# Gate products and squares of a chunked scan on GpSimd in place of VectorE, and five weight splits at other steps of the attention beside it

## What is computed

```python
proj = rms_norm(x, norm_w) @ w_in
z, xbc, dt, q, k, v, g = split(proj)
y = ssd_chunked_scan(xs, dt, A, bm, cm) + d_skip * xs     # 256 x 1024
y = y * silu(z)                                           # gate product
y = rms_norm(y.reshape(256, 4, 256), ssd_norm_w)          # squares, sums, root
o = dilated_attention(q, k, v) * silu(g)                  # 8 heads, 3 dilations
x = x + concat([y, o]) @ w_out                            # 1536 x 1024
```

## Time and profile before

| what | before |
|---|---|
| median of 3 runs | 1747.39 us |
| lowest, highest run | 1747.34, 1750.71 us |
| the profiled execution, its own time | 1747.27 us |
| its span in the trace | 1745.2 us |
| TensorE busy | 1704.9 us, 98% of the span |
| VectorE busy | 1254.9 us, 72% |
| ScalarE busy | 961.1 us, 55% |
| GpSimd busy | 22.7 us, 1% |

### The profile page before, as it was taken

The page is one execution under the profiler, slowest core; times in us unless marked ns, Lnnn a source line. Parts: engine busy times, 40 slices in busy tenths (PEclk is TensorE's granted clock), DMA queues, the critical chain, the costliest instruction groups (busy, mean ns, idle before and its releaser), DMA issues. The chain is left out here.

```text
span 1745.2 us, 28417 instructions
## 1 busy us (share of the span) xinstructions
PE 1704.9 (98%) x10546; PEld 1487.7 (85%) x10546; DVE 1254.9 (72%) x2290; ACT 961.1 (55%) x1622; POOL 22.7 (1%) x21
## 2 busy tenths in 40 slices
PE   7999999999999999999999999999999999989998
PEld 6888899998888888888899988888888987878887
DVE  6666777567876667666776667866677799696775
ACT  5444555666555446444655665555556555574474
POOL 1000000000000000000000000000000000000000
PEclk9999999999999999999999999999999999999999
DMA  7545555634545554455555544455544444203531
GB/s 315 188 180 191 203 196 181 234 141 182 183 184 201 192 205 169 181 186 201 192 191 221 190 145 182 181 183 194 200 182 181 181 162 164 109 38 145 211 115 61
DMA packets 29904, 311.59 MB, mean 179 GB/s; under 512 B 3312, under 2 KB 3696, under 8 KB 4848
## 3 DMA queue, kind: packets, MB, share of 16 engines
q1 hardware_dynamic: 28944, 307.13, 47.5%
q0 software_dynamic: 864, 3.15, 0.5%
HBM read 309.21 MB, written 1.05 MB: 178 GB/s over the span
## 5 line engine op out<-in xcount | busy, mean ns | idle before, releaser
L505 ACT ACTIVATE region_r<-ring 128x1024 fp32r<-128x1024 f32 x505 | 525.1, 1054 | 360.1 <-PE psum L923 335.5
L511 DVE TENSOR_TENSOR ring_r<-ring,region_r 128x1024 fp32r<-128x1024 f32 x496 | 592.4, 1221 | 128.6 <-ACT region_r L505 123.6
L923 PE MATMUL psum<-xs_r,region_r 128*128 128x256 f32 (+2 forms) x3160 | 580.0, 331 | 3.2 <-ACT region_r L505 1.4
L923 PEld LDWEIGHTS psum<-xs_r,region_r 128*128 128x128 f32 (+1 forms) x3160 | 466.4, 188 | 65.8 <-issue 7.7
L923 PE MATMUL psum<-region_r 128*128 128x512 f32 (+3 forms) x1056 | 330.7, 381 | 0.0
L923 PE MATMUL psum<-xs_r,ring_r 128*128 128x256 f32 x2344 | 317.6, 278 | 0.0
L923 PEld LDWEIGHTS psum<-xs_r,ring_r 128*128 128x128 f32 x2344 | 303.9, 188 | 15.8
L923 PE MATMUL psum<-region_r,xs_r 128*128 128x512 f32 (+2 forms) x1056 | 272.8, 351 | 6.0 <-DVE region L2771 3.0
L923 PEld LDWEIGHTS psum<-region_r 128*128 128x128 f32 (+2 forms) x1056 | 193.1, 185 | 36.4 <-DVE region_r L2441 0.6
L923 PEld LDWEIGHTS psum<-region_r,xs_r 128*128 128x128 f32 x1056 | 185.6, 191 | 34.5 <-DVE region L2771 4.3
L923 PE MATMUL psum<-ring_r,region_r 128*128 128x512 f32 (+1 forms) x472 | 169.5, 376 | 0.0
(11 more groups left out here) (253 smaller groups left out, 1538.2 us busy)
## 6 DMA issues: line engine op xcount, KB each, us to landing
ring<-in_weights SPq DMA_DIRECT2D x192, 1536.0 KB, 6.3
gpost<-in_posts POOLq DMA_DIRECT2D x6, 512.0 KB, 4.5
cst<-in_const SPq DMA_DIRECT2D x1, 1165.0 KB, 22.7
PTs<-in_mem SPq DMA_DIRECT2D x1, 1024.0 KB, 5.6
x<-in_x SPq DMA_DIRECT2D x1, 1024.0 KB, 8.1
out<-x SPq DMA_DIRECT2D x2, 512.0 KB, 2.6
pars<-in_par SPq DMA_DIRECT2D x1, 368.0 KB, 6.1
p<-in_par SPq DMA_DIRECT2D x1, 206.0 KB, 22.7
```

The source lines that it names most:

```text
L505: eng.activation(unit.high, unit.like_high(unit.raw), ACT.Copy).then_inc(h_ready, 1)
L511: eng.tensor_tensor(unit.like_high(unit.low), unit.like_high(unit.raw), unit.high.bitcast(F32), ALU.subtract)\
L923: ins = pe.matmul(bank, lhsT, rhs, start=start, stop=stop)
```

## The change

The two gate products and the two squares leave VectorE's steps 1 to 4 and become four instructions of GpSimd, behind its last low part. GpSimd waits for all four banks of the scan to be emptied and for `z_ready`; a square waits for its product by the new semaphore `y_gated`, and VectorE's sum of squares at step 5 waits for the new `y_squared` in place of its own. The low parts of units 2 to 6, made at steps 6 to 10 before, are made at steps 3, 4, 6, 7 and 8.

```diff
@@ GpSimd, behind its last low part
             lows([U_EVEN + AHEAD_N - 1])
+
+            all_emptied(pool, [("scan", j) for j in range(4)])
+            pool.wait_ge(z_ready, 1)
+            for i in range(NT):
+                pool.tensor_tensor(ysb[:, i], ysb[:, i], Z[:, i, :], ALU.mult).then_inc(y_gated, 1)
+            for i in range(NT):
+                pool.wait_ge(y_gated, i + 1)
+                pool.tensor_tensor(yt[:, i], ysb[:, i], ysb[:, i], ALU.mult).then_inc(y_squared, 1)
@@ VectorE, y_steps
                 if s == 0:
                     scanned(1)
-                elif s in (1, 2):
-                    if s == 1:
-                        all_emptied(dve, [("scan", j) for j in range(4)])
-                    dve.wait_ge(z_ready, 1)
-                    own(dve.tensor_tensor(ysb[:, s - 1], ysb[:, s - 1], Z[:, s - 1, :], ALU.mult))
-                elif s in (3, 4):
-                    own.settle()
-                    own(dve.tensor_tensor(yt[:, s - 3], ysb[:, s - 3], ysb[:, s - 3], ALU.mult))
                 elif s == 5:
-                    own.settle()
+                    dve.wait_ge(y_squared, NT)
                     dve.tensor_reduce(stat[:, 0, 0:8], yt.rearrange("p i (g d) -> p (i g) d", g=4), AX.X, ALU.add)\
                         .then_inc(y_sq, 1)
...
-                if 6 <= s <= 9:
-                    low_part(dve, U_EO + s - 4)
+                if s in (3, 4, 6, 7, 8):
+                    low_part(dve, U_EO + (3, 4, 6, 7, 8).index(s) + 2)
                 elif s == 10:
                     mixed_low(8)
-                    low_part(dve, U_EO + 6)
```

More of the change, by code:

```diff
@@ L756, in build @@
         y_sq, y_std, y_ready = sem("y_sq"), sem("y_std"), sem("y_ready")
+        y_gated, y_squared = sem("y_gated"), sem("y_squared")
         trig_in, trig_done = sem("trig_in"), sem("trig_done")
```

## The result

The changed kernel takes 1750.43 us (median of 9 runs, 1750.15 to 1754.97) against 1747.77 for the kernel before in the same comparison (9 runs, 1747.18 to 1750.71): a ratio of 1.0022, 95% interval 1.0014 to 1.0030, or +2.7 us. Its profiled execution took 1753.06 us, with a span of 1751.1; it is already 2.34 us late where the dilated attention begins, which is the difference of two executions and not the change's. So the lengths of one piece are compared from here on: from the start of TensorE's scores of head 0 to its first transposes of the scan output. It contains all that the change touches but the low part of step 10, which stood right behind it; behind it both traces have 179.9 us to their end. In the kernel before it runs from 1525.55 to 1565.34, 39.79 us; after, from 1527.89 to 1571.20, 43.31: **+3.52 us**.

A forecast was written before the change was run, and what follows sets the result against it. TensorE, busy 98% of the span, was taken as the bound, with 4.4 us idle to win. Turns made head 1's transposes 4.06 us late; partial recovery left +2.6 on 1747.39, so 1750.0 us, range 1745.2 to 1751.7.

The forecast's parts named there:

- step 4: Dilated attention: VectorE's scalings and GpSimd's four instructions wait for each other's whole instructions; TensorE ends +2.6 us late.
- rival A: GpSimd also blocks the 128x2 scaling L2547 between front and pair: +3.2 to +3.7 us, about 1751.0; chance 0.23.
- step 3: GpSimd's four added instructions, 2.35 us each, 9.4 in all, start 0.08 us after the last scan bank is emptied.
- The first pair: Head 0's two L2568 scalings wait for GpSimd's first and second products, ending at 1535.09 us instead of 1532.48.
- The second pair: Head 1's two L2568 scalings wait for both GpSimd squares, ending at 1540.23 us; TensorE's transposes come 4.06 us late.
- VectorE's lateness in the middle: VectorE 3.43 us late from head 4's front on; TensorE's idle 0.79 us at head 7's scores shrinks to 0.16.
- The end: TensorE's idle 0.83 us before the stretch's end disappears, as VectorE's last scaling ends at 1567.57 and TensorE's outputs at 1567.94.
- Rival B: Scalings take no turn with GpSimd, or the pair keeps the path: faster within 0.2%, 1745.1 to 1746.1 us; chance 0.20.
- C: Nearly all 4.4 us of TensorE's idle time in the dilated attention goes: 1743.0 to 1743.8 us; chance 0.04.
- D: VectorE's late steps fall into TensorE's pace, so the time does not change, +-0.5 us; chance 0.05.

The follow-up runs named there:

- run with uncut products: Fitted run with GpSimd's two gate products as whole 128x1024 tiles behind the last scan bank, VectorE squaring: 1750.03 us, ratio 1.0013.
- the fitted one: The change with gate products on GpSimd cut into four halves placed early, squares back on VectorE, low parts at steps 6 to 8 and the end: 1746.23 us.
- relief alone: The change with the gate products and squares left out altogether, made by no engine: 1747.14 us, ratio 0.9994.
- clock kept up: The change plus 18 identity transposes on TensorE while it waits ahead of head 0's transposes: 1751.78 us, ratio 1.0027.
- the run with one column: The change with the 128x2 scaling of the maxima written as two of 128x1 in the dilated attention: 1752.48 us, ratio 1.0019.
- the one with the low parts back: The change with VectorE's low parts of output weights back at steps 6 to 10: 1753.51 us, ratio 1.0040.
- the one with less work on VectorE: Fitted run with ScalarE squaring and summing tile 1 of the scan output, VectorE's low parts up to two steps sooner: 1744.91 us, ratio 0.9986.
- VectorE late alone: Fitted run plus two overwritten reductions on VectorE ahead of head 0's pair of scalings: 1749.04 us, ratio 1.0009.
- the transposes put in: 18 identity transposes in TensorE's wait, added to the change (1751.78 us), to uncut products (1749.48) and to VectorE late alone (1747.03).

## Why the prediction was right, and where not

The number was right: 1750.0 forecast, 1750.43 measured, +2.6 against +2.7 (interval +2.4 to +5.2). The ratio, 1.0022, lies just over the 0.2% that the prediction took as its bound, so on the side to which it gave 0.27 and not 0.68, with the interval over both. The mechanism of step 4 holds: whole instructions of GpSimd and VectorE take turns, scalings too. The run with uncut products against the fitted one shows it with the amount held the same. But the sum came out by errors that cancel, which is luck: the course was the first half of rival A, whose own sign (L2547 of head 1 at about 1 us) came true with 1.08, and the piece's +3.52 lies in A's +3.2 to +3.7, though by the half clock that A did not have.

| the piece from head 0's scores, us | length | against before |
|---|---|---|
| before | 39.79 | |
| relief alone | 38.09 | -1.70 |
| GpSimd's turns added, clock kept up | 42.45 | +2.66 |
| the change | 43.31 | +3.52 |

- **The start (step 3).** GpSimd takes up the signal of the last emptied bank 0.26 us after it (1532.10 to 1532.36), not 0.08. Products take 2.36, as taken from the earlier trace rows; the squares, which read one tensor twice, 2.07 and not 2.35. So the second square ends at 1541.11 - 2.34 = 1538.77 in the time of the trace of before, where the forecast had 1539.89.
- **The first pair (step 4).** It should have waited for the rest of the first product and, between its two scalings, for the second. The 128x2 scaling before it was held, which is the first half of rival A; that cost 0.91 us and let the second product ahead of the pair. Idle 4.49 us, not 2.5. The prediction's reason against A, that two columns hardly need a second path, is what failed: two do, one doesn't (0.21 us in the run with one column).
- **The second pair.** Forecast: held by both squares, transposes of head 1 4.06 us late. Shown: free, since the squares had ended 0.12 us before it. The whole loss sits at head 0; the transposes of head 1 are 4.46 late (15.14 against 10.68 us from the scores of head 0), 3.62 in the run with the clock kept up.
- **VectorE's lateness in the middle.** Forecast 3.43, with the idle 0.79 shrinking to 0.16. Shown: as late as TensorE, 4.4 us (the sum of squares at 1554.23, less 2.34, against 1547.47), and 0.75 left. The step set VectorE's front of head 4 at the very end of its scores; it starts 0.58 us behind them (scores to 1547.10, front at 1547.68), and 0.58 in the relief alone too (1541.95, 1542.53). In the trace of before 0.63 lay between (1540.29, 1540.92), but there VectorE's own square filled it. With 0.58 put in, VectorE is as late as TensorE and the idle 0.79 cannot shrink. What the 0.58 us are was not tried.
- **The end.** The idle 0.83 us disappears, as forecast, in every run but the one with the low parts back, where it stays.
- **The half clock** stood nowhere in the prediction: 0.86 us of the 3.52.

Without it the piece has grown by 2.66 us, the forecast's 2.6: TensorE is 3.62 us late at head 1's transposes and not 4.06, and makes up 0.96 of it and not 1.46.

Of the signs that the prediction named, these came: the pair of head 0 far over 0.48 us a scaling, the gap at the end gone, no wait for the squares. These did not: the later instructions of GpSimd at 2.5 us or more (2.36 and 2.07), the pair of head 1 held, the idle time of 2.5 us twice (4.49 once, and nothing at head 1).

**Rival B**'s walk of the relief alone gave -2.3 where -1.70 was measured: head 3's scores come 0.74 us sooner and not 0.9, and the idle 0.79 keeps 0.74. **C** fell with it: with four instructions off VectorE and nothing on GpSimd's side, 2.5 us of idle time remain (0.76, 0.74, 1.04). **D** is excluded by the interval.

What stays open: the medians scatter about the difference of the pieces by up to 2.1 us (most in the run with the low parts back, whose interval of +4.5 to +9.4 leaves its piece's +4.08 just out; the other nine hold theirs). Other parts of the program vary from one execution to the next, also by the clock (below).

## What to carry to other kernels

Before work goes to GpSimd beside VectorE, list which of VectorE's instructions would share a path with it and on which of them another engine waits; then cut and place GpSimd's instructions between those: here the same two products cost 4.8 us (2.3 of them half clock) or nothing. A blocked instruction shows as a long busy one, not as a wait, so compare durations of the same form, not idle times. Take work off a nearly full engine only as far as the next pace allows: 4.6 us off VectorE was worth 1.7.

## What was unexpected of the hardware

Idle time of TensorE costs more than itself. At this place all five traces with an idle piece of 4.49 us (twice), 2.86, 2.75 or 2.68 us have a stretch at a granted clock of 0.50 with it, 3.4 us long in three and 6.8 in two (2.86 and 2.68). It began between 0.8 us before the end of the idle piece and 1.7 us behind it. The seven traces with 1.50 or 0.76, or with 2.39, 0.76 or 0.63 behind 18 small transposes, have none. It cost 0.9, 1.6 and 2.3 us, by its length and by how much later waiting absorbed. The timed runs agree: the mean granted clock was 0.999 or more in 41 of 74 runs of the kernel before, 6 of 11 of the relief alone, 10 of 11 of the fitted one and 7 of 11 of the one with less work on VectorE, but in none of 9 of the change, none of 5 with the low parts back, none of 7 with the smaller scaling, 1 of 11 with the uncut products and 4 of 12 with VectorE late alone. With the transposes put in, none of 9 became 2 of 6, 1 of 11 became 4 of 11 and 4 of 12 became 8 of 12. Such stretches also come elsewhere in some executions, so the clock is not at its full level throughout, although the section on the metric says so: it is 0.50 for 3.4 us from 960.7 and from 1476.1 us in the trace of before, and for as long around 322 and 971 us in that of the change. The trace of the change with TensorE kept busy has none of these. What sets those was not tried.
